# Where the low parts of eight sample columns lie in a split-precision decoder layer

## The reference

```
h   = layer_norm(x)
rq,rk,rv,rg, fq,fk,fv, ff, gr,gf = split(h @ w_in)
o_r = group_norm(retention(rope(rq), rope(rk), rv)) * silu(rg)
o_f = softmax attention with forget gates (pages of past keys and values for the samples)
mix = (sigmoid(gr) * (o_r @ w_ret_proj) + sigmoid(gf) * (o_f @ w_fox_proj)) @ w_out
x1  = layer_norm(ALPHA * h + mix)
y   = layer_norm(ALPHA * x1 + (silu(x1 @ w1) * (x1 @ w3)) @ w2
                 + sigmoid(x1 @ w_pg) * (p @ w_pe))
```

## Time and profile before

| what | us |
|---|---|
| median of 3 runs | 1942.47 (1941.87 to 1943.74) |
| the profiled execution, its span | 1944.3 |
| PE busy in it | 1859.9 |
| DVE busy | 1050.1 |
| ACT busy | 793.6 |
| POOL busy | 148.5 |

### The profile page before, as it was taken

One profiled execution on the slowest core, in us unless ns is written; L12 is line 12 of the kernel. 1 busy time (PEld: TensorE's weight loads), 2 busy tenths in 40 slices (PEclk: granted clock), 3 DMA queues, 4 the chain that ended last, 5 costly groups with the idle time before them and its releaser, 6 DMA issues.

```text
span 1944.3 us, 39410 instructions
## 1 busy us (share of the span) xinstructions
PE 1859.9 (96%) x14346; PEld 1754.6 (90%) x14346; DVE 1050.1 (54%) x2097; ACT 793.6 (41%) x930; POOL 148.5 (8%) x262
## 2 busy tenths in 40 slices
PE   5999999999899999999978999999999999999996
PEld 4999998888777877889978999999999999999995
DVE  5444575864767666447556554444444444444554
ACT  2444434433433443334335445555433343443333
POOL 3330101111121112000000000000000000000000
PEclk9999999999999999899988999999999999999999
DMA  5555677787799899545533555555555555555551
GB/s 157 151 160 158 215 247 227 249 273 228 260 344 315 294 333 334 166 149 183 181 106 125 180 177 181 182 182 179 177 179 178 183 180 182 177 179 173 178 179 45
DMA packets 318257, 386.18 MB, mean 199 GB/s; under 512 B 16376, under 2 KB 293368, under 8 KB 317784
## 3 DMA queue, kind: packets, MB, share of 16 engines
q1 hardware_dynamic: 286832, 287.48, 47.7%
q0 software_dynamic: 28352, 95.84, 14.3%
q10 hardware_dynamic: 2992, 1.79, 0.4%
HBM read 371.21 MB, written 13.84 MB: 198 GB/s over the span
## 4 chain that ended last, share of the span: by engine, by line
PE 72%; DVE 4%; issue 2%; DMA 2%; ACT 1%; POOLq 0%; DVEq 0%; ACTq 0%; POOL 0%
PE acc L506 22%; PE acc L511 22%; PE acc L507 22%; PE X L631 2%; DMA page<-in_cache_v 2%; PE X L756 1%; PE X L819 1%; DVE pagesum L1249 1%; PE X L620 1%; PE X L641 0%; DVE uT L1497 0%; DVE wlo L452 0%; PE X L613 0%; ACT uT L1078 0%; ACT whi L447 0%
## 5 line engine op out<-in xcount | busy, mean ns | idle before, releaser
L452 DVE TENSOR_TENSOR wlo<-raw,whi 128x1024 fp32r<-128x1024 f32 (+1 forms) x552 | 658.9, 1202 | 658.5 <-ACT whi L447 651.5
L447 ACT ACTIVATE whi<-raw 128x1024 fp32r<-128x1024 f32 (+1 forms) x552 | 568.8, 1037 | 683.2 <-PE acc L511 680.8
L506 PE MATMUL acc<-x_hi,whi 128*128 128x264 f32 x1664 | 415.8, 285 | 10.3 <-DVE x_lo L1506 6.8
L507 PE MATMUL acc<-x_lo,whi 128*128 128x264 f32 x1664 | 415.2, 285 | 0.0
L506 PE MATMUL acc<-hT_hi,whi 128*128 128x264 f32 x1408 | 366.8, 295 | 0.0
L507 PE MATMUL acc<-hT_lo,whi 128*128 128x264 f32 x1408 | 356.8, 288 | 0.0
L506 PEld LDWEIGHTS acc<-x_hi,whi 128*128 128x128 f32 x1664 | 313.8, 189 | 11.4 <-issue 7.2
L507 PEld LDWEIGHTS acc<-x_lo,whi 128*128 128x128 f32 x1664 | 315.3, 189 | 0.0
L506 PEld LDWEIGHTS acc<-hT_hi,whi 128*128 128x128 f32 x1408 | 270.5, 192 | 41.5 <-issue 37.9
L507 PEld LDWEIGHTS acc<-hT_lo,whi 128*128 128x128 f32 x1408 | 271.4, 193 | 0.1
L511 PE MATMUL acc<-x_hi,wlo 128*128 128x264 f32 x1664 | 239.7, 286 | 0.0
(11 more groups left out here) (300 smaller groups left out, 1727.3 us busy)
## 6 DMA issues: line engine op xcount, KB each, us to landing
raw<-in_w SPq DMA_DIRECT2D x256, 512.0 KB, 3.9
raw<-in_w_in SPq DMA_DIRECT2D x176, 512.0 KB, 4.9
page<-in_cache_k POOLq DMA_DIRECT2D x64, 512.0 KB, 6.2
page<-in_cache_v POOLq DMA_DIRECT2D x64, 512.0 KB, 5.7
raw<-in_w_out SPq DMA_DIRECT2D x32, 512.0 KB, 4.5
raw<-in_w_pg SPq DMA_DIRECT2D x32, 512.0 KB, 3.5
stateS<-in_state_ret POOLq DMA_DIRECT2D x8, 1024.0 KB, 7.9
out_ret_state_sample<-stateS POOLq DMA_DIRECT2D x8, 1024.0 KB, 7.3
```

The lines of the kernel that those rows point to most:

```text
L447: nc.scalar.activation(whi[:, s, 0:k, :], raw[:, s, 0:k, :], ACT.Copy).then_inc(S["hi_made"], 1)
L452: nc.vector.tensor_tensor(wlo[:, s, 0:k, :], raw[:, s, 0:k, :], whi[:, s, 0:k, :].bitcast(F32), ALU.subtract).then_inc(S["lo_made"], 1)
L506: mm(acc[c.acc][:, m, 0:T], w, xh[:, c.kt0 + t, :], start=c.first and t == 0, stop=False)
L507: mm(acc[c.acc][:, m, 0:T], w, xl[:, c.kt0 + t, :], start=False, stop=False)
```

## The change

Each high-part tensor of activations grows from 264 to 272 columns (TW = T + DEC): the 8 new columns hold the low parts of the 8 sample columns. Each low-part tensor shrinks to the 256 prompt columns. The product of high weights with high activations then moves 272 columns and writes the samples' low products to accumulator columns 264 to 271; the product of high weights with low activations moves 256; the third moves 264 as before. Before a group can be read, the accumulator's columns 264 to 271 have to be added to its columns 256 to 263: `sum_group` does this on DVE with two instructions (a copy to `low`, then an addition in PSUM that waits for the copy). In DVE's list it stands right after `split_lo(j+3)` of the iteration whose chunk ends a group, and it waits for that chunk to be multiplied. Readers of the accumulator on ACT and on DVE wait for it (`group_summed`) where they waited for PE. Every place that makes low parts is split in two instructions, one for the prompt columns and one for the sample columns. In F every chunk now waits for all of `hT_lo` with one more POOL instruction, where chunk j waited for its own four tiles.

```diff
+    TW = T + DEC
...
-        hT_hi = place("hT_hi", [P, DT, T], F32R)
-        hT_lo = place("hT_lo", [P, DT, T], F32R)
+        hT_hi = place("hT_hi", [P, DT, TW], F32R)
+        hT_lo = place("hT_lo", [P, DT, SEQ], F32R)
...
+        low = place("low", [P, 2, 2, DEC], F32)
...
-        phF = Phase(plan, 2, heads([FK, FQ, FV], 512, ready=lambda k: ("h_lo", k)))
+        phF = Phase(plan, 2, heads([FK, FQ, FV], 512, ready=lambda k: ("h_lo", DT + 1)))
...
+        def group_summed(eng, ph, it, j):
+
+            eng.wait_ge(summed[ph.chunks[j].acc], ph.sums(it, j, 2))
+
+        def sum_group(dve, ph, it, j):
+
+            if not ph.chunks[j].last:
+                return
+            i = ph.chunks[j].acc
+            group_done(dve, ph, it, j)
+            nc.vector.tensor_copy(low[:, i, :, :], acc[i][:, :, T:TW]).then_inc(summed[i], 1)
+            dve.wait_ge(summed[i], ph.sums(it, j, 1))
+            nc.vector.tensor_tensor(acc[i][:, :, SEQ:T], acc[i][:, :, SEQ:T], low[:, i, :, :], ALU.add).then_inc(summed[i], 1)
...
-                        mm(acc[c.acc][:, m, 0:T], w, xh[:, c.kt0 + t, :], start=c.first and t == 0, stop=False)
-                        mm(acc[c.acc][:, m, 0:T], w, xl[:, c.kt0 + t, :], start=False, stop=False)
+                        mm(acc[c.acc][:, m, 0:TW], w, xh[:, c.kt0 + t, :], start=c.first and t == 0, stop=False)
+                        mm(acc[c.acc][:, m, 0:SEQ], w, xl[:, c.kt0 + t, :], start=False, stop=False)
...
-                        last = mm(acc[c.acc][:, m, 0:T], wlo[:, s, t, m * P:(m + 1) * P], xh[:, c.kt0 + t, :],
+                        last = mm(acc[c.acc][:, m, 0:T], wlo[:, s, t, m * P:(m + 1) * P], xh[:, c.kt0 + t, 0:T],
...
                     if phG.chunks[j].last:
                         g, ac = j // 4, phG.chunks[j].acc
-                        group_done(act, phG, it, j)
+                        group_summed(act, phG, it, j)
...
             for it in range(phR.iters):
                 for j in range(len(phR.chunks)):
                     split_lo(dve, phR, it, j + AHEAD)
+                    sum_group(dve, phR, it, j)
...
                 for j in range(len(phG.chunks)):
                     split_lo(dve, phG, it, j + AHEAD)
+                    sum_group(dve, phG, it, j)
                     window("middle", (it, 4), j)
...
-                        link.step(V.scalar_tensor_tensor(out=u, in0=hT_lo[:, ds(k, 2), :].bitcast(F32), scalar=ALPHA, in1=u, op0=ALU.mult, op1=ALU.add))
+                        up, us = uT[:, ds(k, 2), 0:SEQ], uT[:, ds(k, 2), SEQ:T]
+                        V.scalar_tensor_tensor(out=up, in0=hT_lo[:, ds(k, 2), :].bitcast(F32), scalar=ALPHA, in1=up, op0=ALU.mult, op1=ALU.add)
+                        link.step(V.scalar_tensor_tensor(out=us, in0=hT_hi[:, ds(k, 2), T:TW].bitcast(F32), scalar=ALPHA, in1=us, op0=ALU.mult, op1=ALU.add))
...
-                            V.tensor_tensor(x1_lo[:, k, :], uT[:, k, :], x1_hi[:, k, :].bitcast(F32), ALU.subtract).then_inc(S["x1_lo_made"], 1)
+                            V.tensor_tensor(x1_lo[:, k, :], uT[:, k, 0:SEQ], x1_hi[:, k, 0:SEQ].bitcast(F32), ALU.subtract)
+                            V.tensor_tensor(x1_hi[:, k, T:TW], uT[:, k, SEQ:T], x1_hi[:, k, SEQ:T].bitcast(F32), ALU.subtract).then_inc(S["x1_lo_made"], 1)
...
-                nc.gpsimd.tensor_tensor(hT_lo[:, k, :], h32[:, k, :], hT_hi[:, k, :].bitcast(F32), ALU.subtract).then_inc(S["h_lo"], 1)
+                nc.gpsimd.tensor_tensor(hT_lo[:, k, :], h32[:, k, 0:SEQ], hT_hi[:, k, 0:SEQ].bitcast(F32), ALU.subtract).then_inc(S["h_lo"], 1)
+            nc.gpsimd.tensor_tensor(hT_hi[:, :, T:TW], h32[:, :, SEQ:T], hT_hi[:, :, SEQ:T].bitcast(F32), ALU.subtract).then_inc(S["h_lo"], 1)
```

More of the change, by code:

```diff
@@ L133, in group, with sums @@
         return it * self.per[acc] + (self.group0[acc] + before)
+    def sums(self, it, j, k):
+        acc = self.chunks[j].acc
+        before = sum(c.first for c in self.chunks[:j + 1] if c.acc == acc) - 1
+        return it * (2 * self.per[acc]) + (2 * (self.group0[acc] + before) + k)
     def n_kt(self, j):
@@ L196, in layer_kernel @@
         wlo = place("wlo", [P, RING, KT, NC], F32R)
-        hT_hi = place("hT_hi", [P, DT, T], F32R)
-        hT_lo = place("hT_lo", [P, DT, T], F32R)
[L199 to L202, removed]
+        hT_hi = place("hT_hi", [P, DT, TW], F32R)
+        hT_lo = place("hT_lo", [P, DT, SEQ], F32R)
+        orT_hi = place("orT_hi", [P, 8, TW], F32R)
+        orT_lo = place("orT_lo", [P, 8, SEQ], F32R)
+        ofT_hi = place("ofT_hi", [P, 8, TW], F32R)
+        ofT_lo = place("ofT_lo", [P, 8, SEQ], F32R)
         region = top[0]
@@ L281, in layer_kernel @@
         assert after("vr8") <= made["page"][0]
-        mix_hi = place("mix_hi", [P, DT, T], F32R, at=made["stateS"][0])
-        mix_lo = place("mix_lo", [P, DT, T], F32R, at=after("mix_hi"))
+        mix_hi = place("mix_hi", [P, DT, TW], F32R, at=made["stateS"][0])
+        mix_lo = place("mix_lo", [P, DT, SEQ], F32R, at=after("mix_hi"))
         usum = place("usum", [P, 2, T], F32, at=after("mix_lo"))
@@ L287, in layer_kernel @@
         uT = place("uT", [P, DT, T], F32, at=region)
-        x1_hi = place("x1_hi", [P, DT, T], F32R, at=made["orT_hi"][0])
-        x1_lo = place("x1_lo", [P, DT, T], F32R, at=after("x1_hi"))
+        x1_hi = place("x1_hi", [P, DT, TW], F32R, at=made["orT_hi"][0])
+        x1_lo = place("x1_lo", [P, DT, SEQ], F32R, at=after("x1_hi"))
         assert after("x1_lo") <= region
@@ L298, in layer_kernel @@
         assert after("ytok8") <= made["orT_hi"][0]
-        g_hi = place("g_hi", [P, HF2, T], F32R, at=after("uT"))
-        g_lo = place("g_lo", [P, HF2, T], F32R, at=after("g_hi"))
+        g_hi = place("g_hi", [P, HF2, TW], F32R, at=after("uT"))
+        g_lo = place("g_lo", [P, HF2, SEQ], F32R, at=after("g_hi"))
         assert after("g_lo") <= made["usum"][0]
@@ L326, in layer_kernel @@
           lnv_ps lnstd_made x1_made x1_hi_made x1_lo_made r_res g_made g_hi_made g_lo_made scaled x1_act_made
-          yT_ps y_tok y8_tok acc0_free acc1_free pool_step sp_step""".split()
+          yT_ps y_tok y8_tok acc0_free acc1_free acc0_sum acc1_sum pool_step sp_step""".split()
         S = {n: sem(n) for n in names}
         free = [S["acc0_free"], S["acc1_free"]]
+        summed = [S["acc0_sum"], S["acc1_sum"]]
         W = {k: a[k] for k in ("w_in", "w_ret_proj", "w_fox_proj", "w_out", "w1", "w3", "w2", "w_pg", "w_pe")}
@@ L872, in _ @@
                 act.wait_ge(S["h_made"], k + 1)
-                A(hT_hi[:, k, :], h32[:, k, :], ACT.Copy).then_inc(S["h_hi"], 1)
+                A(hT_hi[:, k, 0:T], h32[:, k, :], ACT.Copy).then_inc(S["h_hi"], 1)
                 if k % 6 == 5 and k // 6 < 1:
@@ L885, in _ @@
             act.wait_ge(S["pT_ps"], 1)
-            A(pT_hi[:, :, :], X[:, 1:3, 0:T], ACT.Copy).then_inc(S["p_hi"], 1)
+            A(pT_hi[:, :, 0:T], X[:, 1:3, 0:T], ACT.Copy).then_inc(S["p_hi"], 1)
             def fox_values(it):
@@ L1059, in _ @@
                         k = it * 4 + j // 2 * 2
-                        A(mix_hi[:, ds(k, 2), :], gate[:, ds(k, 2), 0, :], ACT.Copy).then_inc(S["mix_hi_made"], 1)
+                        A(mix_hi[:, ds(k, 2), 0:T], gate[:, ds(k, 2), 0, :], ACT.Copy).then_inc(S["mix_hi_made"], 1)
             with act.Fori(0, phO.iters) as it:
@@ L1088, in _ @@
                         act.wait_ge(S["x1_act_made"], q * 2 + k % 4 - 1)
-                    A(x1_hi[:, k, :], uT[:, k, :], ACT.Copy).then_inc(S["x1_hi_made"], 1)
+                    A(x1_hi[:, k, 0:T], uT[:, k, :], ACT.Copy).then_inc(S["x1_hi_made"], 1)
             with act.Fori(0, phP.iters) as it:
@@ L1107, in _ @@
                             act.wait_ge(S["g_made"], it + (half * HF2 // 2 + 1))
-                            A(g_hi[:, ds(it * 2, 2), :], gact[:, :, :], ACT.Copy).then_inc(S["g_hi_made"], 1)
+                            A(g_hi[:, ds(it * 2, 2), 0:T], gact[:, :, :], ACT.Copy).then_inc(S["g_hi_made"], 1)
                 with act.Fori(0, down.iters) as it:
@@ L1161, in _ @@
                 split_lo(dve, phF, 0, j)
-            dve.wait_ge(S["h_lo"], DT)
+            dve.wait_ge(S["h_lo"], DT + 1)
             dve.wait_ge(S["ff_ps"], 1)
@@ L1191, in _ @@
                     split_lo(dve, phF, it, j + AHEAD)
+                    sum_group(dve, phF, it, j)
                     if it == 1 and j == 2:
@@ L1280, in rope @@
                 ac = ph.chunks[j].acc
-                group_done(dve, ph, it, j)
+                group_summed(dve, ph, it, j)
                 z = acc2(ac)
@@ L1448, in _ @@
                         dve.wait_ge(S["mix_hi_made"], it * 2 + (n + 1))
-                        V.tensor_tensor(mix_lo[:, k, :], gate[:, k, 0, :], mix_hi[:, k, :].bitcast(F32), ALU.subtract)\
+                        V.tensor_tensor(mix_lo[:, k, :], gate[:, k, 0, 0:SEQ], mix_hi[:, k, 0:SEQ].bitcast(F32), ALU.subtract)
```

(7 more changed lines are left out.)

42 lines of the change are left out of this document (23 added, 19 removed).

## The result

The changed kernel takes 1976.38 us (median of 4 runs, 1973.55 to 1978.78) against 1942.17 (1941.68 to 1943.74). The ratio is 1.0171, with an interval of 1.0157 to 1.0185. The profiled span grew from 1944.3 to 1974.2 us. The forecast was 1962, with a range from 1934 to 1981.

A forecast was written before the change was run, and what follows sets the result against it. The prediction took PE's three matmul lines, 66% of the span, as the bound. Its terms, 0 for the stream, 5.1 in R, 11.2 in G and 3.0 from O on, sum to 19.3 us: 1962 on the median, range 1934 to 1981.

The forecast's parts named there:

- The pages: G, positions 7 to 11: the wait for a late value page grows by 2.1 us in all four iterations.
- From O to the end: O, layer norm, P and the last group: sums and small partner instructions of the splits cost 3.0 us.
- G, position 0: Start of G's iterations two to four: chunk 15's gate comes later and `scd` has no slack, 0.43 us each.
- R: Stage R: four waits off DVE's chain grow 0.43 us each, two delays of ACT's silu cost 1.7 each; 5.1 us.
- The two larger terms: R, chunk 31 and the end: ACT's silu loads its table only after the sum, 2 x 1.7 us.
- `probT` in G: G, positions 3 to 5: ACT's gate comes 2.6 us later against 2.1 of slack; PE waits 0.5 us, three times.
- the stream: PE's matmuls throughout: pace unchanged at a floor of 117 to 122 ns set by the weight load; 0 us.
- L507's pace fell: Sign in the matmul stream: a fall in the pace of L507 would show the prediction wrong.
- The floor is asymmetric: Rival on the stream: 272 columns pay 125.3 ns, 256 stay at 122; +14.4 us, so 1976; chance 0.12.
- The short matmul sheds its 12 ns: Rival on the stream: the 256-column matmul drops towards 106.7 ns; -52 us at most, about 1910 with costs; chance 0.18.
- The slack swallows it: Rival on the waits: pages land sooner and slack meets ACT's later split; 5 us or less, 1944 to 1947; chance 0.10.
- the clock: G, bounds only: a chunk at 220 instead of 122 ns after longer idle, 2.4 us more, up to 9.4 in four iterations.

The follow-up runs named there:

- the columns alone: The changed kernel without its sums: operands of 272, 256 and 264 columns, readers waiting for the last matmul as before; 1936.87 us, ratio 0.9969.
- the run with the longer loop: The kernel before with four pairs of DVE instructions that do nothing useful added per iteration of G's loop; 1950.25 us, ratio 1.0033.
- the shorter columns: The changed kernel without its sums, with operands of 264, 256 and 256 columns instead of 272, 256 and 264; 1915.56 us, ratio 0.9846.
- the run with both edits: The changed kernel with chunk 7's sum earlier in G and 71 idle DVE instructions ahead of G; 1953.83 us, ratio 1.0057.

## Why the prediction was right in direction and short by 14 us

*Right.* The pages: 4 x 2.1 = 8.4 forecast, 8.3 measured, by the way described. From O to the end: 3.0 forecast, 2.5 by PE's waits. The first layer norm waits 0.6 longer for the last group of O (2.5 to 3.1), then 0.35 for `x1_lo` and what follows it (6.83 to 7.11 and 2.61 to 2.68; 1.2 were forecast), the two `sgt` waits grew by 1.1 together (0.9 to 2.0), the wait for the last group of all by 0.42 (1.54 to 1.96). The rest of the end's 1.5 us is the clock: the 32 matmuls of L819 took 10.28 us at a granted clock of 0.71 where they had taken 8.91 at 0.82. The second instruction of `x1_lo` costs little, as forecast: four pairs take 1.66 us to the start of what follows (1052.36 to 1054.02) where four single ones took 1.38 (1021.24 to 1022.62).

```profile
1052.36 0.43 DVE L1516 TENSOR_TENSOR x_lo<-uT,x_hi 128x256 fp32r<-128x256 f32 x1 [0.71 <-ACT x_hi L1089]
...
1054.02 1.25 DVE L1507 TENSOR_TENSOR uT<-uT,rstd 128x1056 f32<-128x1056 f32 x1
```

*Wrong: G, position 0.* The step "The gate of chunk 15 is 0.43 later, and `scd` behind it has no slack in iterations two to four: 0.43 each" was too small by a factor of eleven: 4.8 each. It counted the added instructions' durations and not what it means that they lengthen the program. The runs put the cause in the loop's place in DVE's program: it goes when the loop is unrolled or moved, and appears in the kernel before when that loop is moved. With the loop moved, the forecast 0.43 is what is left, in each of the three iterations; the second's:

```profile
581.80 1.04 PE L614 MATMUL X<-cst,scd 128*8 128x128 f32 x8 [0.43 <-DVE scd L1241]
```

*Wrong: R.* 5.1 forecast. The stretch up to G grew by 0.5 with the faster stream in it; by PE's waits it is 0.9: `prodS` 0.6, `scd` 1.0 in three, the late page 0.3, `probT` -1.0. The two larger terms (2 x 1.7) rested on ACT's table load standing behind the wait for the sum. It doesn't there:

```profile
354.57 1.28 ACT L973 ACT_TABLE_LOAD   x1
354.58 1.23 DVE L438 TENSOR_TENSOR wlo<-raw,whi 128x1024 fp32r<-128x1024 f32 x1 [1.65 <-ACT whi L433]
...
355.93 0.18 DVE L457 TENSOR_TENSOR acc<-acc,low 128x16 f32<-128x16 f32 x1
356.14 0.61 ACT L973 ACTIVATE sg<-acc 128x528 f32<-128x528 f32 x1 [0.29 <-DVE acc L457]
...
359.49 1.24 PE L613 MATMUL X<-cst,scd 128*8 128x128 f32 x8 [2.14 <-DVE scd L1238]
```

The load runs at once, until 355.85; the sum is over 0.26 us later, at 356.11. Only the ACTIVATE waits, 0.29 us, and `scd` is missed by 2.14 instead of 1.85. At the end of R the wait grows by as much, from 5.74 to 6.02. In G's loop the load does wait (598.01, 2.64 us for the sum), as assumed for positions 3 to 5. R is written out in Python and G is a loop, so the waits are constants in the one and registers in the other; that this is the reason was not tried. R's wait for `probT` fell from 1.5 to 0.5 instead of growing.

*Hidden: `probT` in G.* 3 x 0.5 forecast, none in the changed kernel. With the stall mended, it stands there: 0.56 in the fence above, 0.59 and 2.15 in the two iterations that follow; in the unrolled run it is 1.79 to 1.87. The wait was rightly foreseen, its size at the lower end, and a larger delay ahead of it covered it.

*Wrong: the stream.* 0 forecast, -6.0 measured by the columns alone; L507's pace fell, which the prediction had named as a sign that it is wrong. The working rightly refused rounding, but then took 117 to 122 ns for a floor set by the weight load. There is none down to 256 columns. The 117 ns divide a whole stretch by 16; by their starts these matmuls lie 111 to 112 ns apart, all but the first two (133). By the starts of all steps at the full clock, the step from L506 to L507 takes 125.1 ns after the change and that from L507 to L506 117.4, against 121.6 and 121.7: sum 242.5 instead of 243.3. The rest of the gain is at the passage from L507 to L511 (116.3 instead of 121.7) and from L511 back to L506 (119.0 instead of 123.6). P and the feed-forward, which hardly wait, became 4.1 us shorter. One chunk of the changed kernel shows the gain: 2.92 us from start to start, median 2.920 against 2.934 before.

```profile
1500.73 0.29 PE L506 MATMUL acc<-g_hi,whi 128*128 128x272 f32 x1
...
1502.66 1.15 PE L511 MATMUL acc<-g_hi,wlo 128*128 128x264 f32 x8
1503.65 0.29 PE L506 MATMUL acc<-g_hi,whi 128*128 128x272 f32 x1
```

The rule that the prediction weighed, of the Trainium skill's "TensorE: Matmul & The Clock Gate", section "LDWEIGHTS (loading the stationary operand)", gives the load of 128 columns 106.7 ns. Both 117.4 ns with 256 columns and 111 to 112 for nearly bare loads lie above that, so the rule does not forbid the gain; the prediction's step from it to a floor at 122 was wrong. Why the shorter operand saves 4.3 ns and the longer costs 3.4 stayed open.

*The rivals.* "The floor is asymmetric" forecast 1976, which is the time measured, and is nevertheless refuted: its mechanism would have made the columns alone slower, and they are faster. A time that fits is no proof of its cause. "The short matmul sheds its 12 ns" was right in sign, at an eighth of its size. "The slack swallows it" holds for R alone.

*Left out of the sum: the clock.* PE's 8.6 us of additional busy time in G were only in the bounds (2.4 us per longer wait). The sum as measured: 0.5 + 31.4 - 0.5 + 1.2 - 4.1 + 1.5 = 30.0, as the span.

*Luck.* That 1976 still lies below the range's end of 1981 is no merit of the working. That end was made of the floor case and 5 us of the clock; what filled it is a stall of 14.3 us in three waits that no part of the prediction names, against which R and the stream came out lower than forecast.

## What to carry to other kernels

An instruction added to a loop that is a few hundred instructions long, or ahead of it, can cost more by where it moves the loop than by its duration: look for "issue" before the first instruction of the body and for more packets on the instruction queue, and move the loop or write it out before blaming the instruction. When an engine takes over a step for another, put it ahead of the waits that this engine already has in its list; the same two instructions cost 8.6 us of page waits in one place and 2.1 a few lines earlier. Here the longer waits were followed by stretches at the lower clock, so price a wait that grows at more than its length.

## What the runs showed of the hardware

- DVE's loop of G: 5.8 to 6.5 us of idle time per return, 15 or 16 more instruction packets of 8 KB, from 302 instructions at place 922 or 923 or 291 at place 943; none from 302 at 994 or 301 at 866. Written out, a packet for 112 to 140 instructions, and no idle time.
- A step of PE with a weight load of its own: 118.1, 122.4 and 125.6 ns for 256, 264 and 272 columns at 2.4 GHz (three runs, L505); 220.0 for 264 at 1.2 GHz.
- An ACT table load ahead of a waiting ACTIVATE ran 1.57 us ahead of it in straight code (354.57 and 356.14) and waited with it in a loop (598.01).
- Not settled: 6 us of the run with the longer loop; 4 us by which the shorter columns gained less than their pace; the 6 us by which the run with both edits lies over its range; how many blocks of its program DVE keeps.
